# A two-block transformer on one core: a modulation sum moved behind the head norms, a norm factor spread without a diagonal tile, and a second weight block split inside the norms

## The reference

```python
for l in range(2):                                   # first stack
    sh1, sc1, g1, sh2, sc2, g2 = split(silu(c) @ w_mod[l] + b_mod[l])
    u = rms_norm(h, norm1_g[l]) * (1 + sc1) + sh1
    y = even_mixer(u, uc, ...) if l == 0 else pool_mixer(u, ...)
    h = h + g1 * y
    u = rms_norm(h, norm2_g[l]) * (1 + sc2) + sh2
    h = h + g2 * (relu(u @ w1) ** 2 @ w2)
u = rmsnorm(h, norm_mix_g)                           # second block
ya, yb = sliding_window_sink_attention(...) @ wa, hgrn2_branch(...) @ wb
h = h + (sigmoid(gate_a) * ya + sigmoid(gate_b) * yb) @ w_out
u = rmsnorm(h, norm_ffn_g)
h = h + (silu(u @ w_gate) * (u @ w_up)) @ w_down
out = rmsnorm(h, norm_final_g)
```

## Time and profile before

| | |
|---|---|
| median of three runs | 2226.83 us (2220.97, 2226.83, 2227.38) |
| the profiled execution | 2228.16 us, of which the span is 2226.4 us |
| mean granted clock of TensorE in it | 0.961 |
| PE busy | 2092.7 us, 94% of the span |
| weight loads of PE | 1690.4 us, 76% |
| DVE / ACT / POOL busy | 923.1 (41%) / 684.5 (31%) / 794.6 (36%) us |
| HBM read | 218.80 MB, 99 GB/s over the span |

### The profile page before, as it was taken

The page is one execution under the profiler, slowest core; times in us unless marked ns, Lnnn a source line. Parts: engine busy times, 40 slices in busy tenths (PEclk is TensorE's granted clock), DMA queues, the critical chain, the costliest instruction groups (busy, mean ns, idle before and its releaser), DMA issues. The chain is left out here.

```text
span 2226.4 us, 25643 instructions
## 1 busy us (share of the span) xinstructions
PE 2092.7 (94%) x10180; PEld 1690.4 (76%) x10180; DVE 923.1 (41%) x1516; ACT 684.5 (31%) x912; POOL 794.6 (36%) x240
## 2 busy tenths in 40 slices
PE   7969999899999979999998879999997998999998
PEld 3856577688888768888886648888885876888886
DVE  1426665858577544323222480124444123212122
ACT  2312352312212242222223472245553233222122
POOL 2312124343444434444453104433230453444444
PEclk9889999899999979999998999999996999999999
DMA  8153304235253223222222103221210321223221
GB/s 344 44 160 102 137 1 170 114 151 215 95 217 115 109 76 108 97 98 94 94 75 96 43 1 112 93 78 60 73 58 19 114 85 67 99 92 111 94 76 38
DMA packets 42772, 224.17 MB, mean 101 GB/s; under 512 B 12736, under 2 KB 13376, under 8 KB 17216
## 3 DMA queue, kind: packets, MB, share of 16 engines
q1 hardware_dynamic: 42688, 223.01, 27.7%
HBM read 218.80 MB, written 2.10 MB: 99 GB/s over the span
## 5 line engine op out<-in xcount | busy, mean ns | idle before, releaser
L832 POOL TENSOR_TENSOR wl<-raw,wh 128x2048 fp32r<-128x2048 f32 (+1 forms) x155 | 711.4, 4590 | 1261.1 <-ACT wh L476 1261.1
L913 PE MATMUL bank<-uh,wh 128*128 128x512 f32 x1480 | 590.0, 399 | 24.8 <-POOL wl L832 9.6
L915 PE MATMUL bank<-uh,wl 128*128 128x512 f32 x1480 | 582.6, 394 | 0.0
L914 PE MATMUL bank<-ul,wh 128*128 128x512 f32 x1480 | 582.4, 393 | 0.0
L476 ACT ACTIVATE wh<-raw 128x2048 fp32r<-128x2048 f32 (+1 forms) x155 | 292.9, 1890 | 589.6 <-PE bank L915 589.6
L913 PEld LDWEIGHTS bank<-uh,wh 128*128 128x128 f32 x1480 | 282.2, 191 | 95.1 <-issue 23.6
L913 PE MATMUL bank<-ah,wh 128*128 128x512 f32 x816 | 322.6, 395 | 6.4 <-DVE al L1748 6.4
L914 PEld LDWEIGHTS bank<-ul,wh 128*128 128x128 f32 x1480 | 282.0, 191 | 59.7 <-issue 1.7
L915 PEld LDWEIGHTS bank<-uh,wl 128*128 128x128 f32 x1480 | 281.4, 190 | 60.1
L915 PE MATMUL bank<-ah,wl 128*128 128x512 f32 x816 | 320.9, 393 | 0.0
L914 PE MATMUL bank<-al,wh 128*128 128x512 f32 x816 | 318.2, 390 | 0.0
(11 more groups left out here) (213 smaller groups left out, 2081.9 us busy)
## 6 DMA issues: line engine op xcount, KB each, us to landing
raw<-in_w SPq DMA_DIRECT2D x64, 1024.0 KB, 6.6
mraw<-in_w_modr SPq DMA_DIRECT2D x32, 1024.0 KB, 4.9
raw<-in_w_gu SPq DMA_DIRECT2D x22, 1024.0 KB, 4.9
raw<-in_w_hg SPq DMA_DIRECT2D x16, 1024.0 KB, 4.9
modf<-in_w_modf SPq DMA_DIRECT2D x8, 1024.0 KB, 17.3
raw<-in_w_in SPq DMA_DIRECT2D x8, 1024.0 KB, 16.5
raw<-in_w_out SPq DMA_DIRECT2D x8, 1024.0 KB, 5.0
mmid<-in_w_modr SPq DMA_DIRECT2D x8, 1024.0 KB, 4.9
```

Source lines behind the costliest of these rows:

```text
L832: pool.tensor_tensor(wl[:, b % 2, 0:nk], raw[:, b % RAW, 0:nk], f32(wh[:, b % 2, 0:nk]), ALU.subtract).then_inc(split_lo, 1)
L913: pe.matmul(out, ah_, bh, start=first, stop=False)
L914: pe.matmul(out, ah_, bl, start=False, stop=False)
L915: return pe.matmul(out, al_, bh, start=False, stop=last)
```

## The change

1. `mod_sum(3)` moves on DVE from before the head norms to the point (4, 1), between head norms 3 and 4; `mod_store(1)` to (5, 1); on PE `mod_columns(1)` moves from behind the first half of block 2 to behind the first half of block 5. SP's list is not changed.
2. The norm factor: DVE no longer makes `diag`. PE waits for the reciprocal and does four fp32 products of 128 columns, each with one factor column broadcast as the stationary operand and the identity as the moving one.
3. In the norms "mlp0", "pool", "mix2" and "ffn" ACT's split of the second block is made in two parts of four chunks each, before the highs of chunks 2 and 3; POOL's split follows after the second part. In the loops behind them ACT's `split(j + 1)` ahead of block j's evictions becomes `split(j + 2)` behind them. So the last iteration of the pool loop splits mlp1's second block, and the last one of the aq/akv loop splits the second block of ga, ahead of the attention.

```diff
@@ act.split
-            def split(b, q=0, per=0):
+            def split(b, q=0, per=0, part=None):
                 s = b % RAW
+                if part == 1:
+                    nk = chunks_of(b, per)
+                    act.activation(wh[:, b % 2, nk // 2:nk], raw[:, s, nk // 2:nk], ACT.Copy).then_inc(split_hi, 1)
+                    return
...
                 nk = chunks_of(b, per)
+                if part == 0:
+                    act.activation(wh[:, b % 2, 0:nk // 2], raw[:, s, 0:nk // 2], ACT.Copy)
+                    return
                 act.activation(wh[:, b % 2, 0:nk], raw[:, s, 0:nk], ACT.Copy).then_inc(split_hi, 1)
@@ act.highs
                 for k in range(KC):
+                    if beside is not None and k in (2, 3):
+                        split(beside, part=k - 2)
@@ act, the mlp loop (the pool, aq and ffn loops alike)
                     for j in range(8):
-                        split(b0 + j + 1, q, 8)
...
+                        if not last or j < 7:
+                            split(b0 + j + 2, q, 8)
+                        if last and j >= 4:
+                            squares(after, h, (2 * (j - 4), 2 * (j - 4) + 1))
...
-            highs("mix2", None, uh)
+            highs("mix2", None, uh, beside=FIRST["aq"] + 1)
@@ act
-            gates(FIRST["ga"], V_BGA)
+            gates(FIRST["ga"], V_BGA, done=1)
@@ pe.norm_sum
-                pe.wait_ge(diag_ready, i + 1)
-                pe.matmul(rms[:, 0:n], ones_v, diag[:, 0:n // P, :].rearrange("p a n -> p (a n)"), start=True, stop=True).then_inc(rms_full, 1)
+                pe.wait_ge(rstd_ready, i + 1)
+                for a in range(n // P):
+                    last = pe.matmul(rms[:, P * a:P * a + P], rc[:, 1, a:a + 1].to_broadcast([P, P]), ident, start=True, stop=True)
+                last.then_inc(rms_full, 1)
@@ pe.beside
-                    if half == 0 and b == 2:
+                    if half == 0 and b == 5:
                         mod_columns(1)
@@ dve.norm_factor
                 dve.wait_ge(root_ready, i + 1)
+                if i:
+                    dve.wait_ge(rms_full, i)
                 dve.reciprocal(rc[:, 1, 0:c], rc[:, 0, 0:c]).then_inc(rstd_ready, 1)
-                dve.wait_ge(rstd_ready, i + 1)
-
-                dve.scalar_tensor_tensor(diag[:, 0:c, :], ident.rearrange("p (a n) -> p a n", a=1).to_broadcast([P, c, P]), float(P),
-                                         rc[:, 1, 0:c].rearrange("p (a n) -> p a n", n=1).to_broadcast([P, c, P]), ALU.mult, ALU.mult).then_inc(diag_ready, 1)
@@ dve
             mod_sum(2)
-            mod_sum(3)
-            mod_store(1)
             for b in range(2, 8):
                 for half in (-1, 0, 1):
+                    if (b, half) == (4, 1):
+                        mod_sum(3)
                     if (b, half) in HN_AFTER:
                         hn_scale(HN_AFTER[b, half])
+                    if (b, half) == (5, 1):
+                        mod_store(1)
```

More of the change, by code:

```diff
@@ L492, in root, with highs @@
                 act.activation(rc[:, 0, 0:n // P], norm_banks(name)[0][:, 0:n // P], ACT.Sqrt, bias=eps_col, scale=P / D).then_inc(root_ready, 1)
-            def highs(name, shift, hi, n=S):
+            def highs(name, shift, hi, n=S, beside=None):
                 i = NORM[name]
                 for k in range(KC):
+                    if beside is not None and k in (2, 3):
+                        split(beside, part=k - 2)
                     act.wait_ge(t_ready, 8 * i + k + 1)
@@ L608, in group @@
                     for j in range(8):
-                        split(b0 + j + 1, q, 8)
[L610 to L614, removed]
+                        for half in range(2 if j < 4 else 0):
                             bi, m = bank_of(b0 + j, half), 2 * j + half
@@ L623, in mlp @@
                 group(3, True)
-                squares(after, h, (6, 7))
                 root(after)
-            highs("mlp0", lambda k: mod(0, 3, k), uh)
+            highs("mlp0", lambda k: mod(0, 3, k), uh, beside=FIRST["mlp0"] + 1)
             mlp(0, "pool")
-            highs("pool", lambda k: mod(1, 0, k), uh)
+            highs("pool", lambda k: mod(1, 0, k), uh, beside=FIRST["pool"] + 1)
             b0 = FIRST["pool"]
             for g in range(FG):
-                split(b0 + g + 1)
                 for half in range(2):
@@ L638, in _ @@
                     act.activation(zt[:, g, 2 * half:2 * half + 2, :], bank[bi][:].rearrange("p (a n) -> p a n", a=2), ACT.Copy).then_inc(bank_free[bi], 1)
+                split(b0 + g + 2)
             squares("mlp1", h, range(KC))
@@ L649, in _ @@
             for j in range(5):
-                split(b0 + j + 1)
                 for half in range(2 if j < 4 else 1):
@@ L655, in _ @@
                     act.activation(out, bank[bi][:], ACT.Identity, bias=vec[:, col:col + 1]).then_inc(bank_free[bi], 1)
+                split(b0 + j + 2)
             def exp2(i):
@@ L681, in _, with gates @@
             o2_high(KC - 1)
-            def gates(first, col, done=0):
+            def gates(first, col, done):
                 for j in range(8):
@@ L797, in _ @@
             root("ffn")
-            highs("ffn", None, uh)
+            highs("ffn", None, uh, beside=FIRST["ffn"] + 1)
             b0 = FIRST["ffn"]
@@ L812, in _ @@
                 for j in range(12):
-                    split(b0 + j + 1, q, 12)
                     if j < 8 and j % 2 == 0:
                         gate_units(j, j, q, 12, 8)
+                    split(b0 + j + 2, q, 12)
             for j in range(10):
-                if j < 9:
-                    split(b0 + 24 + j + 1)
                 if j < 6 and j % 2 == 0:
                     gate_units(24 + j, 16 + j)
-                if j > 6:
-                    squares("final", h, (2 * (j - 7), 2 * (j - 7) + 1))
-            squares("final", h, (6, 7))
+                if j < 8:
+                    split(b0 + 24 + j + 2)
+                if j >= 6:
+                    squares("final", h, (2 * (j - 6), 2 * (j - 6) + 1))
             root("final")
```

5 lines of the change are left out of this document (2 added, 3 removed).

## The result

| | before | after |
|---|---|---|
| median | 2227.11 us (4 runs, 2220.97 to 2229.11) | 2189.39 us (4 runs, 2187.26 to 2190.91) |
| profiled execution, its span | 2228.16, 2226.4 us | 2189.44, 2187.7 us |
| mean granted clock of TensorE | 0.961 | 0.969 |
| PE busy / POOL busy | 2092.7 / 794.6 us | 2081.5 / 795.7 us |

The medians differ by 37.7 us. The ratio is 0.9835 with a 95% interval of 0.9814 to 0.9855, which is 32 to 41 us. The forecast was 21 us faster, 2206 us, with a range of 2200 to 2212 that its rivals A and C stretch to 2195. The direction was right, the size was not: 2189.4 lies outside the range and outside its stretched end.

What follows compares the result with a forecast made beforehand. PE, busy 94% of the span, was taken as the bound, through its waits and lower clock. 14.0 + 5.5 + 5.5 - 4.0 = 21.0 us off 2228.2, less 1.3 for the median: about 2206 us, range 2200 to 2212.

Steps and rivals of the forecast that it cites:

- rival A: `load(8)` is hardly late, as table loads issue faster in their new place; 2199 us, chance 0.12.
- Rival C: DVE/POOL collisions cost little since POOL waits: attention's 4.0 gone, up to 4.5 more in the norms; 2197 us, chance 0.12.
- The stop for the moved sum: PE's stop at `mod_columns(1)` from 112.5 us goes and the clock comes back: 20.8 us gained.
- The late `load(8)`: SP's tail waits for the moved sum, so block 8's weights come late: 4.6 us of wait and 2.2 of clock lost.
- The chain behind: Late weights delay ACT's split of block 8, head norm 8 and PE's (7, 1): 4.6 us, plus 2.2 of clock.
- The norm factor: All eight norms lose DVE's `diag` and one hop from PE's path: 5.5 us gained.
- The equal price of the two ways to spread the factor: Per norm, eight 128-column matmuls cost PE the same as two of 512: 2.05 against 2.08 us at half clock.
- The second block: Earlier second-block splits remove PE's waits for `wl`, less collisions with DVE's low parts: 5.5 us gained, bounds 2 and 10.
- The early gate split: POOL's split ahead of the sliding-window attention holds DVE's first small SBUF op: 4.0 us lost, bounds 0 and 4.6.
- The clock beyond the stop: Clock changes away from the removed stop and the new one before (7, 1) were given no term.
- The terms' own bounds: Better ends: 20.8 for the moved sum with `load(8)` in time, 10 for the second block, 0 for the early gate split.

Runs made afterwards that it cites:

- Part 1 alone: Kernel before with only the fourth modulation sum, its columns and its store moved: 2206.38 us, against 2226.56 for before.
- the run that brought it about: Changed kernel with the two 1 MB DFT loads put behind SP's wait for the fourth sum: 2195.01 us, 5.6 slower than the changed kernel.
- The run with two pieces: Changed kernel with each POOL split of a full block made in two instructions of four chunks instead of one of eight: 2186.93 us.
- the fastest kernel: Changed kernel with POOL's splits in four pieces of two chunks and without the gate block's split ahead of the attention: 2180.99 us, ratio to before 0.9808.
- part 3 alone: Kernel before with only the second-block splits moved, without the gate block's split ahead of the attention: 2212.47 us, against 2226.56 for before.

## Why the prediction was wrong, step by step

- **The stop for the moved sum** (18.9 + 2.8 - 0.9 = 20.8): right. Part 1 alone showed 20.7 in the trace and 20.2 in the median. DVE's four ops took 3.10 us in the gap and head norm 4 was not late.
- **The late `load(8)` (-4.6 - 2.2)**: this step failed. The tail's 21.8 us were taken from rows 5 as a property of these loads; the runs showed 16.8 in the new place and 21.4 once the DFT loads stand ahead again. The forecast gave rival A 0.12 although the argument for it was written down: in the old place the DFT loads stood just ahead. The chain behind, with its price, was confirmed by the run that brought it about. A had asked for 15 us of table loads to save all of it; 15.8 were enough, and the margin is small: the weights landed at 171.3 and ACT wanted them at 172.59. With this step put right the forecast's own sum gives 2199.
- **The norm factor (5.5)**: its waits right, 5.6. The equal price of the two ways to spread the factor holds, 2.08 and 2.08 us at half clock and 1.16 against 1.12 at full. The figures that the Trainium skill gives in "TensorE: Matmul & The Clock Gate", section "Back-to-back issue gap", spoke by the prediction's estimate for 0.4 us more per norm; measured are 0.0 and 0.04 for these fp32 products.
- **The second block (5.5)**: right in kind, low by 1.8. The waits for `wl` fell by 10.5 and the low parts gave back 3.2, 7.3 net; alone, part 3 had 5.3 net. The held low part took 4.30 us, as worked out (1187.88 to 1192.2), but PE's wait for it was 1.0 to 1.1 us and not 1.4; and the pool mixer's wait for `wl` fell by 0.9, not 0.3.
- **The early gate split (-4.0)**: 3.3 in the wait, and 1 to 2 in the median of the kernel without it.
- **Rival C**, that POOL is the one that waits, held for the moved sum's last op, but not for the two collisions that it was priced on. Who waits goes by who began first, as the Trainium skill has it ("SBUF — State Buffer", section "Who interferes with whom"), and the trace agrees in both directions: POOL took up to 5.16 us where DVE had begun, and the low part took 4.30 and the attention's small op 3.99 where POOL had. There DVE came second, as the prediction argued. The run with two pieces shows that the hold lasts one instruction.
- **The clock beyond the stop (costed at nothing)**: this is the second step that failed, a term that was put at nothing without a reason. The forecast treated stretches at half clock as fixed to their places, except where a stop was added or removed, and so had 1.6 us of clock in all. The first pair of profiles had 11.2, the mean of three of each kernel 7.2. Of the first pair's 11.2 the HGRN part alone has 6 (24 us at half clock against 12), and the kernel before ran it with 12 in its third profile too. Which of the parts takes how much away is not shown, since single profiles of one kernel differ by as much, and why a stretch falls stays open.

Waits: 4.6 for `load(8)`, 1.8 for the second block, 0.7 for the attention, 0.8 from the first modulation loads, which landed 1 us earlier in this execution, and 0.3 in small ones: 8.2. Clock: 9.6, of which 2.2 belong to `load(8)` and about 4 to the luck of the two profiles. Single executions of before take from 2217.5 to 2230 us, some 6 us to either side of their middle. A range that had let the clock vary by this would have reached down from 2195 to 2189. The terms' own bounds, all taken at their better ends (20.8 + 5.5 + 10 + 0 = 36.3), reach 2190.5, but that would have been luck: DVE was held, as the forecast said, and the rest was clock.

Left open: why the HGRN part has 12 to 15 us at half clock in some executions and 19 to 25 in others. The three profiles of the changed kernel and that of the fastest kernel are at the low end; those of the kernels without the early split, with two pieces and without part 2 are at 22 to 25, and so are part 1 alone, part 3 alone and two of before's three. One wait in that part goes with it, PE's for DVE's `ex`: 3.6 us in every profile at the low end, 2.6 to 2.8 in all others. It can be the cause or the effect. Three profiles of each kernel don't tell a rule from chance, and no run was made that sets it.

## What to carry to other kernels

When a group of DMAs moves in the queue, don't move its issue time with it: look at what was in flight ahead of it in the old place and what will be in the new one. A GpSimd pass over SBUF that is put beside VectorE work costs the next VectorE op whose tensors all lie in SBUF the rest of that instruction, so put it where the next VectorE ops read PSUM, or cut the pass into pieces. And on a kernel that lives at the edge of the clock's two levels, take more than one profile of the kernel before: some 4 us of this forecast's miss are the luck of one pair of profiles, and 4.9 of the 8.5 us between two executions of one kernel are a single stage falling on one level or the other.

## What was not expected of the hardware

- Sixteen table loads of 96 KB in rows of 48 elements take 15.8 to 15.9 us to issue with nothing just ahead, 19.9 to 20.3 with two 1 MB loads just ahead; most of the difference is in the two table loads that are issued before the second of these has landed.
- A VectorE op on two elements per partition (0.17 us) is held for 3.99 us by a GpSimd pass over SBUF just as a 512-element one is, and a cast of one input is too (4.82 instead of 0.43 us); two such ops in a row are held twice if the pass consists of two instructions (1.83 and 2.26 us).
- Back-to-back GpSimd instructions let a VectorE op in between them: with four pieces of 1.37 us the low parts took 1.0 us instead of 4.30.
- One unchanged kernel ran the same window of 60 us at a mean clock of 0.72, 0.74 and 0.83 in three executions, with PE's waits within 1.2 us of each other in total.
